# All four chunks' keys turned through VectorE and scratch memory, and two more gate pairs ahead of the projections, in a hybrid decoder layer

## The chip, the cores and the metric

One NeuronCore of a Trainium2 chip runs the whole program. The metric is the device time of one execution in microseconds (us). The profiled execution has a span (first to last recorded event) and, around it, a little time that is counted but not in the span.

## The reference

One decoder layer with model width 1024 is computed for a prompt of 2048 tokens and for 8 decode rows (one token each, with cached keys, values and state). Cut to what matters:

```
h    = rms_norm(x) * (1 + scale) + shift
proj = h @ w_in -> qa, ka, va, za, qb, fb, ib, zb
ya   = window_attention(rope(norm(qa)), rope(norm(ka)), va) * silu(za)      8 heads of 64, window 128
f    = lb + (1 - lb) * sigmoid(fb);  k = (1 - lb) * sigmoid(-fb)            4 heads of 128
per chunk:  o = (q * decay) @ S + A @ v;   S = decay_end * S + (k * decay_to_end)^T @ v
yb   = rms_norm(o) * silu(zb)
y    = sigmoid(h @ w_merge_a) * (ya @ w_proj_a) + sigmoid(h @ w_merge_b) * (yb @ w_proj_b)
out  = x + gate * (y @ w_out)
```

The outputs are the rows of both batches, the last 128 keys and values and the state S of each.

## The kernel before

**Passes, units, halves.** The prompt is done in four passes (`it` 0 to 3) of 512 tokens, each four chunks of 128. A pass is a list of 68 units (`UNITS`, line 36): products that fill one of two PSUM banks D0 and D1 in turn. Units 0 to 7 give q, k and v by token, then come four each of `za`, `f`, `qb`, `ib` and `zb` (8 to 27), then the list of `_merges()` (28 to 59), and eight units of the output projection (60 to 67). `ga j` and `gb j` are the gate units of output block j, `pa j` and `pb j` the projections of ya and yb. Each product is three matmuls (high by high, low by high, high by low part, lines 787 to 793), so a unit has 24 of them, a `pa` or `pb` unit 12. TensorE does a unit in two halves; half n stands for unit n // 2, half n % 2. Between halves it does the small tasks that a hand-written table puts there (`put`, `at_half`, lines 142 to 155), in four further PSUM banks XA to XD. Every engine walks the same table in the same order (line 998 on TensorE), does its own part of each task, and waits by semaphores.

**The recurrence's tasks.** After `level` 6 (unit 27) the decayed keys lie in `kk` with the key dimension on the partitions. `st` needs them the other way round. Two ways are in the kernel:

- Chunks 0 and 1: the task `KT` (line 971) turns a chunk with four TensorE transposes in units 28 and 29; ScalarE copies it to `kst` (line 1175).
- Chunks 2 and 3 (half 1, `KEYS_TURNED`): the task `kD` (line 1606) turns `kk` in place in blocks of 32 x 32 on VectorE. SyncE stores that half to the scratch memory `zk` (event `ks`, line 578) and reads it back with the blocks in exchanged places into `k_turned` (event `kl`, line 582, four loads).

Then for each chunk `o` (line 975, output) and `st` (line 986, state update) run on TensorE in banks XB and XA; VectorE adds to the state (line 1603), ScalarE copies `o` to `kk` and sums its squares (line 1180). `onorm` (line 1609) normalizes two chunks and turns them in blocks; SyncE takes them through scratch memory too (events `os`, `ol`). `yD` (line 1619) gates them, `yT` splits them in a high part (ScalarE, line 1222) and a low part (POOL, line 1782), which `pb 0` waits for (line 769). In pass 0 and 1 the constants O_AT, ON_AT, YD_AT, YT_AT give halves, KS_AT to OL_AT give unit numbers, equal in every pass.

**Weights.** A 512 KB block per unit is loaded by SyncE into one of three raw buffers (`weights`, line 535), split into a high part by ScalarE (line 1015) and a low part by POOL (line 1766). The unit at whose second half a block is split is planned (`SPOT`, line 114). SyncE issues block n once block n-3 has its low part and, where block n-3 takes part in a burst, once that burst is done. SyncE's queue is in order: its other transfers are events with a unit number as key, and an event is issued just before the block n with key <= max(SPOT[n-3], BURST_AT[n-3]) (line 688). An event that waits holds up all weight blocks behind it.

**Decode rows.** Their products use the raw blocks in bursts on TensorE in bank XD (task `bu`, lines 832 to 855; groups of four blocks, two blocks per burst, at BURST_AT). A burst waits for the landing of its blocks. One burst is that of ga1 and gb1, in the middle of unit 29 of pass 0. Sums follow one unit later (`sx`, VectorE and ScalarE). In pass 0 the cached keys and values of the decode rows are loaded (event `ckv`, line 636) into a buffer that ga1 and gb1's tanh used before, so it waits until VectorE has left pb1:

```
s.full(0, "PV", 3)
s.wait_ge("s_rows", 1)
s.unit_left(0, "pb", 1)
```

The keys are then turned by TensorE (`sT`, line 871) and used (`sS` to `sO`).

Of the kernel before, what the change touches and what calls it, by code (L numbers as in the profile page):

```python
# [16 lines left out]
P, KT, NT = 128, D // 128, TB // 128  # L17
HB = 4
# [8 lines left out]

def _merges():

    out = [(c, j) for j in range(5) for c in ("ga", "gb")]  # L30
    for j in range(8):
        out += [("pa", j), ("pb", j)] + [(c, {2: 5, 3: 6, 5: 7}[j]) for c in ("ga", "gb") if j in (2, 3, 5)]
    return out


# [94 lines left out]
        assert kind in ("q", "k", "v", "out") or _prev < _it * NU + FIRST_UNIT[_b] + (1 if _n in EARLY else 0), (_n, _prev)  # L130


KEYS_TURNED = (1,)
O_AT, ON_AT, YD_AT, YT_AT = (57, 59, 61, 63), (60, 64), (65, 66, 69, 70), (66, 67, 70, 71)
KS_AT, KL_AT, OS_AT, OL_AT = (28, 28), (28, 28), (30, 32), (31, 32)

AHEAD = {0: (), 1: (5, 7), 2: (1, 3, 5, 7), 3: (1, 3, 5, 7)}
AHEAD_AT = {1: 18, 3: 24, 5: 29, 7: 34}
# [22 lines left out]
for it in range(NIT):  # L161
    if it == 0:
        put(0, 3, 0, "gm", 0, "XA")
        put(0, 4, 1, "late", 0)
        put(0, 8, 0, "gb", 0, "XB")
        put(0, 8, 1, "gS", 0, "XC")
        put(0, 30, 0, "srow", 0)
    if it < 2:
        for _n, _g in enumerate(GROUPS[it]):
            for _b in _g:  # L170
                _s = BURST_AT[it * NB + _b] - it * NU
                if it * NB + _b in PAIR.values():
                    continue
                put(it, int(_s), int(2 * _s) % 2, "bu", _b, "XD", (it, "sg", _n))
            SAMPLE_SLOT[(it, _n)] = _s
    put(it, 2 if it else 20, 0, "at0", 0)
    for _t in range(NT):
        put(it, 2 + _t, 0, "qtB", _t, "XB" if _t % 2 else "XA")
        put(it, 6 + _t, 0, "qtA", _t, "XB" if _t % 2 else "XA")
    put(it, 3, 1, "rsk", 0)  # L180
    put(it, 5, 1, "kt", 0, "XA")
    put(it, 7, 1, "rsq", 0)
    for _n in range(8):
        at_half(it, S_AT[_n], "S", _n, None if _n in AHEAD[it] else "XA")
        at_half(it, S_AT[_n] + 1, "norm", _n)
    for _t in range(NT):
        at_half(it, PV_AT[_t], "PVa", _t, "XA")
        at_half(it, PV_AT[_t], "PV", _t, "XB")
        if _t < 3:
            at_half(it, PV_AT[_t], "turn", 2 * _t + 2)  # L190
    for _n in AHEAD[it]:
        at_half(it, AHEAD_AT[_n], "scores", _n, "XC", (it, "S", _n))
    if it == 0:
        put(0, 20, 0, "dg", 3, "XA", (0, "dg", 0))
    else:
        for _h in range(HB):
            at_half(it, (38, 38, 38, 40)[_h], "dg", _h, "XC", (it, "dg", 0))
    for _l in range(7):
        at_half(it, 42 + 2 * _l, "level", _l, "XA" if _l % 2 else "XB")
    for _t in range(NT):  # L200
        if _t // 2 not in KEYS_TURNED:
            put(it, 28 + _t, 0, "KT", _t, "XC")
        at_half(it, O_AT[_t], "o", _t, "XB")
        at_half(it, O_AT[_t], "st", _t, "XA")
    for _r in KEYS_TURNED:
        at_half(it, 56, "kD", _r)
    for _r in range(2):
        at_half(it, ON_AT[_r], "onorm", _r)
    for _t in range(NT):
        at_half(it, YD_AT[_t], "yD", _t)  # L210
        at_half(it, YT_AT[_t], "yT", _t)
    if it < NIT - 1:
        for _n, _t in enumerate((2, 3, 0, 1)):
            put(it, (41, 42, 45, 46)[_n], 1, "xst", _t)
        put(it, 48, 1, "rstd", 0)
        put(it, 52, 1, "bc", 0, "XA")
        for _n in range(4):
            put(it, (54, 56, 59, 60)[_n], 1, "xm", _n)
            put(it, (57, 58, 61, 62)[_n], 1, "hh", _n)
    if it == 0:  # L220
        for _n in range(11):
            _s = SAMPLE_SLOT[(0, _n)] + 1
            put(0, int(_s), int(2 * _s) % 2, "sy" if _n in (0, 1, 5) else "sx", _n, "XC")
        put(0, 33, 0, "sQ", 0, "XC")
        for _r in range(2):
            _u = (44, 52)[_r]
            put(0, _u, 0, "sT", _r, "XC"), put(0, _u + 1, 1, "sS", _r, "XC"), put(0, _u + 3, 0, "snorm", _r)
            put(0, _u + 4, 1, "sP", _r, "XC"), put(0, _u + 6, 0, "sO", _r, "XC")
    if it == 1:
        for _b in range(NS):  # L230
            put(1, _b + 1, 0, "vB", _b, "XD")
            put(1, _b + 2, 0, "so", _b, "XC", (1, "so", 0))
        put(1, 10, 1, "srms", 0)
        put(1, 13, 0, "soss", 0, "XC")
        for _n in range(6):
            _s = SAMPLE_SLOT[(1, _n)] + 1
            put(1, int(_s), int(2 * _s) % 2, "sx", _n, "XC")
            if _n >= 4:
                _s += 1 + (_n == 4)
                put(1, int(_s), int(2 * _s) % 2, "sOT", _n - 4, "XC")  # L240
# [13 lines left out]
SUMMED = {a: n + 1 for n, a in enumerate((2, 3, 6, 7, 8, 9, 10))}  # L254

TH = {(c, j): j for c in ("za", "f", "zb") for j in range(4)}
TH.update({(c, j): (4, 6, 0, 2, 8, 0, 2, 0)[j] + (c == "gb") for j in range(8) for c in ("ga", "gb")})
TH_PREV, _last = {}, {}
for _it in range(NIT):
    for _u in UNITS:  # L260
# [71 lines left out]
def build(nc, A, O):  # L332

    ctx = ExitStack()
    with ctx:
# [136 lines left out]
        pb = {}  # L472
# [47 lines left out]
        def _(sp):  # L520
# [26 lines left out]
            for it in range(NIT):  # L547
                b0 = it * NU
                if it < NIT - 1:
                    later.setdefault(b0 + 33, []).append(("xst", it, 0))  # L550
                    later.setdefault(b0 + 43, []).append(("x01", it, 0))
                    later.setdefault(b0 + 48, []).append(("xh", it, 0))
                    later.setdefault(b0 + (50 if it else 59), []).append(("xh", it, 1))
                later.setdefault(b0 + 5, []).append(("vr", it, 0))
# [9 lines left out]
                        later.setdefault(b0 + 60 + t, []).append(("out1", it, t))  # L564
                    later.setdefault(b0 + 64 + t, []).append(("out", it, t))
            later.setdefault(3, []).append(("win", 0, 0))
            later.setdefault(41, []).append(("ckv", 0, 0))
            later.setdefault(50, []).append(("ckv", 0, 1))
            later.setdefault(NU - 1, []).append(("sst", 0, 0))
            for b in range(NS):  # L570
                later.setdefault(NU + b + 2, []).append(("sso", 1, b))
# [134 lines left out]
        def _(pe):  # L706
# [90 lines left out]
            def side(it, task, a, key):  # L797
# [160 lines left out]
                elif task == "PV":  # L958
                    s.wait_ge("p_norm", 8 * it + 2 * a + 2)
                    s.wait_ge("vr", 96 * (it + 1))  # L960
                    for j in range(5):
                        for i in range(4):
# [5 lines left out]
                                         start=j == 0, stop=j == 4)  # L968
                            if (i, j) == (1, 4):
                                s.done(ins, "XA_full")  # L970
                elif task == "KT":
                    s.wait_ge("lvl", 8 * it + 8)
                    for h in range(HB):
                        ins = tr(bank[:, P * h:P * h + P], kk[:, h, P * a:P * a + P], ident[:, :])
                elif task == "o":
                    s.freed(it, "level", 6)
                    s.unit_left(it, "ib", a)
# [6 lines left out]
                        ins = mm(bank[:, P * h:P * h + P], AT[:, h, P * a:P * a + P], ibtok[:, a, P * h:P * h + P],  # L984
                                 start=not more, stop=True)
                elif task == "st":
                    if a < 2:
                        s.freed(it, "KT", a)
                    else:
                        s.wait_ge("kt_in1", 64 * (it + 1))  # L990
                    for h in range(HB):
                        left = kst[:, h, :] if a < 2 else k_turned[:, 1, h, a % 2, :]
                        ins = mm(bank[:, P * h:P * h + P], left, ibtok[:, a, P * h:P * h + P],  # L993
                                 start=True, stop=True)
                if PARTS[key][-1] == (task, a):
                    s.done(ins, f"{b}_full")
# [10 lines left out]
        def _(act):  # L1007
# [114 lines left out]
            def side(it, task, a, key):  # L1122
# [47 lines left out]
                elif task == "S":  # L1170
# [1 line left out]
                        s.wait_ge("smax", 2 * (8 * it + a) + m // 2 + 1)  # L1172
                        fn(p_t[:, m, :], p_t[:, m, :], ACT.Exp, bias=negm[:, m:m + 1], accum_out=rsum[:, m:m + 1])  # L1173
                    s.done(fn(esk, esk, ACT.Exp), "p_exp")
                elif task == "KT":
                    s.full(*key)
                    if a:
                        s.full(it, "st", a - 1)
                    s.free(fn(kst, bank[:, :].rearrange("p (h n) -> p h n", h=HB), ACT.Copy), *key)
                elif task == "o":  # L1180
                    s.full(*key)
                    if it or a:
# [731 lines left out]
```

## Time and profile before

| | |
|---|---|
| median of 3 runs | 1548.65 us (1546.63 to 1549.49) |
| the profiled execution | 1547.77 us |
| its span | 1545.6 us |
| TensorE (PE) busy | 1514.8 us, 98% |
| VectorE (DVE) busy | 824.8 us, 53% |
| ScalarE (ACT) busy | 535.9 us, 35% |
| POOL busy | 828.8 us, 54% |

In the rows PE is the matmul side of TensorE and SPq the queue of SyncE. Times are in us from the start of the span where a row begins with one, `x` is a count, and what follows the last bar or stands in brackets is idle time of that engine just before, with what ended it. L983 is line 983 of the kernel. A matmul's duration overlaps the next one's start, so what one costs is read from start to start.

### The profile page before, as it was taken

How to read it: one execution, taken by the hardware profiler on the slowest of the kernel's cores; microseconds unless marked ns; L12 is line 12 of the kernel's file. 1: busy time of each engine (PE TensorE's matmuls, PEld its weight loads, DVE VectorE, ACT ScalarE, POOL GpSimd, SP SyncE). 2: the span in 40 equal slices, each digit the busy share in tenths (PEclk: the TensorE clock that was granted, in tenths of full speed). 3: DMA queues.
4: the chain of work that ended last, by engine and by line, in shares of the span. 5: the costliest groups of instructions: out<-in, count | busy, mean ns of one | idle time of the engine just before them, and what ended most of it. 6: DMA issues, size and time to landing. Idle time of an engine off the chain costs nothing.

```text
span 1545.6 us, 31555 instructions
## 1 busy us (share of the span) xinstructions
PE 1514.8 (98%) x12936; PEld 1232.8 (80%) x12936; DVE 824.8 (53%) x1971; ACT 535.9 (35%) x1112; POOL 828.8 (54%) x1074
## 2 busy tenths in 40 slices
PE   6999999999999999999999999999999999999998
PEld 3777788777887777887779878888888977788886
DVE  5766465236578856434444774642453775642123
ACT  4334323443313432334231452243432352243330
POOL 1525433658854633366683482447795372437671
PEclk9999999999999999999999999999999999999999
DMA  9612213534463311443343331345543231244351
GB/s 365 234 42 85 82 57 94 166 127 160 163 208 113 108 59 59 133 138 136 122 166 124 101 113 42 95 119 171 176 165 136 77 110 56 71 125 124 106 170 58
DMA packets 119047, 191.52 MB, mean 124 GB/s; under 512 B 57198, under 2 KB 74951, under 8 KB 118120
## 3 DMA queue, kind: packets, MB, share of 16 engines
q1 hardware_dynamic: 118480, 189.34, 37.3%
q8 instruction: 102, 1.67, 0.4%
q14 instruction: 41, 0.34, 0.1%
q10 hardware_dynamic: 424, 0.17, 0.0%
HBM read 169.13 MB, written 18.25 MB: 121 GB/s over the span
## 4 chain that ended last, share of the span: by engine, by line
PE 93%; DVE 3%; SPq 1%; issue 1%; DMA 1%; ACT 1%; DVEq 0%
PE ps_D L793 55%; PE ps_D L790 25%; PE ps_XCD L855 1%; PE ps_XB L931 1%; SPq L524 1%; PE ps_XA L956 1%; PE ps_XA L967 1%; PE ps_XA L993 1%; PE ps_XB L984 1%; PE ps_XB L983 1%; PE ps_XA L931 1%; DMA th_t<-in_w_ada 1%; PE ps_XB L967 1%; PE ps_XCD L956 0%; PE ps_XCD L866 0%
## 5 line engine op out<-in xcount | busy, mean ns | idle before, releaser
L1766 POOL TENSOR_TENSOR w_lo_t<-w_raw,w_hi_t 128x256 fp32r<-128x256 f32 x920 | 685.2, 778 | 588.3 <-ACT w_hi_t L1015 588.0
L793 PE MATMUL ps_D<-h_hi_t,w_hi_t 128*128 128x512 f32 x1024 | 409.1, 399 | 0.0
L793 PE MATMUL ps_D<-h_lo_t,w_hi_t 128*128 128x512 f32 x1024 | 399.4, 390 | 0.0
L793 PE MATMUL ps_D<-h_hi_t,w_lo_t 128*128 128x512 f32 x1024 | 399.3, 390 | 0.0
L1015 ACT ACTIVATE w_hi_t<-w_raw 128x1024 fp32r<-128x1024 f32 x232 | 240.0, 1051 | 116.1 <-PE ps_D L790 62.0
L793 PEld LDWEIGHTS ps_D<-h_hi_t,w_hi_t 128*128 128x128 f32 x1024 | 192.2, 188 | 48.0 <-issue 10.0
L793 PEld LDWEIGHTS ps_D<-h_hi_t,w_lo_t 128*128 128x128 f32 x1024 | 192.2, 188 | 41.3
L793 PEld LDWEIGHTS ps_D<-h_lo_t,w_hi_t 128*128 128x128 f32 x1024 | 192.5, 188 | 36.9
L790 PE MATMUL ps_D<-w_hi_t,h_hi_t 128*128 128x384 f32 (+1 forms) x384 | 141.4, 368 | 1.4 <-DVE yf_t L1400 1.0
L790 PE MATMUL ps_D<-w_hi_t,h_lo_t 128*128 128x384 f32 (+1 forms) x384 | 136.5, 355 | 0.0
L790 PE MATMUL ps_D<-w_lo_t,h_hi_t 128*128 128x384 f32 (+1 forms) x384 | 136.3, 355 | 0.0
L790 PE MATMUL ps_D<-w_hi_t,y_hi_t 128*128 128x512 f32 x256 | 100.2, 391 | 2.2 <-issue 2.2
L790 PE MATMUL ps_D<-w_hi_t,y_lo_t 128*128 128x512 f32 x256 | 99.6, 389 | 0.0
L790 PE MATMUL ps_D<-w_lo_t,y_hi_t 128*128 128x512 f32 x256 | 99.6, 389 | 0.0
L790 PEld LDWEIGHTS ps_D<-w_hi_t,h_hi_t 128*128 128x128 f32 x384 | 72.6, 189 | 12.0 <-issue 4.9
L1514 DVE TENSOR_TENSOR qq<-qq,ff 128x1024 f32<-128x1024 f32 x28 | 40.8, 1458 | 70.5 <-PE ps_XB L931 47.1
L1173 ACT ACTIVATE p_or_hf<-p_or_hf,sm 128x160 f32<-128x160 f32 x128 | 53.3, 418 | 68.8 <-DVE sm L1561 67.4
L790 PEld LDWEIGHTS ps_D<-w_hi_t,h_lo_t 128*128 128x128 f32 x384 | 72.6, 189 | 5.1 <-issue 0.5
L790 PEld LDWEIGHTS ps_D<-w_lo_t,h_hi_t 128*128 128x128 f32 x384 | 72.5, 189 | 5.3
L1452 DVE TENSOR_TENSOR acc_or_kst<-ps_D,gate_bc 128x512 f32<-128x512 f32 x32 | 22.1, 692 | 99.6 <-PE ps_D L790 99.6
L1097 ACT ACTIVATE th_t<-ps_D,bm_half 128x512 f32<-128x512 f32 x40 | 27.6, 690 | 132.5 <-PE ps_D L793 132.5
L1603 DVE SCALAR_TENSOR_TENSOR state<-state,ff,ps_XA 128x128 f32<-128x128 f32 x64 | 17.9, 342 | 79.2 <-PE ps_XA L993 79.2
(390 smaller groups left out, 2338.5 us busy)
## 6 DMA issues: line engine op xcount, KB each, us to landing
w_raw<-in_w_blocks SPq DMA_DIRECT2D x232, 512.0 KB, 3.4
xr<-in_x_prompt SPq DMA_DIRECT2D x16, 512.0 KB, 5.1
x_or_AT<-in_x_prompt SPq DMA_DIRECT2D x14, 512.0 KB, 5.0
out_dram<-xr SPq DMA_DIRECT2D x12, 512.0 KB, 2.9
z_o<-kk SPq DMA_DIRECT2D x8, 512.0 KB, 3.1
x_or_AT<-in_x_turned SPq DMA_DIRECT2D x3, 1024.0 KB, 5.7
p_or_hf<-in_x_turned SPq DMA_DIRECT2D x3, 1024.0 KB, 5.7
z_k<-kk SPq DMA_DIRECT2D x4, 512.0 KB, 4.7
```

The source lines that it names most:

```text
L524: s.done(sp.dma_start(dst, src, **kw), name, by=16)
L790: ins = mm(bank[:, 0:P * nb].rearrange("p (n c) -> p n c", c=P), a[:, k, P * j:P * j + P], w[:, s0:s0 + nb, k, :], start=go, stop=end)
L793: ins = mm(bank[:, :], w[:, s0, k0 + k, :], a[:, k, :], start=go, stop=end)
L931: ins = mm(bank[row:row + left, m * col:m * col + m], kk[:, h, c + 32 * g:c + 32 * g + left], right, start=True, stop=True)
L967: ins = mm(dst[DH * g:DH * g + DH], val[:, DH * g:DH * g + DH], PT[r, g, :, 32 * j:32 * j + 32], start=j == 0, stop=j == 4)
L1015: s.done(fn(w_hi[:, SLOT[n % NB]], w_raw[:, n % NRAW], ACT.Copy), "w_hi")
L1097: s.leave(fn(dst, bank[:, :], ACT.Tanh, scale=0.5, bias=bm_half[:, c:c + 1]), it, u)
L1173: fn(p_t[:, m, :], p_t[:, m, :], ACT.Exp, bias=negm[:, m:m + 1], accum_out=rsum[:, m:m + 1])
L1452: leave(tt(acc[:, 0:w], bank[:, 0:w], gate_bc[:, c0:c0 + w], ALU.mult), it, u)
L1514: s.done(tt(qr, qr, fl[:, :, :, 0:1].broadcast_to(shape), ALU.mult))
L1603: ins = stt(state[:, h, :], state[:, h, :], ff[:, h, P * a:P * a + 1], bank[:, P * h:P * h + P], ALU.mult, ALU.add)
L1766: ins = g_.tensor_tensor(w_lo[:, c, k:k + 2], w_raw[:, n % NRAW, k:k + 2], f32(w_hi[:, c, k:k + 2]), ALU.subtract)
```

## The change

It does four things. The merge list puts ga5 and gb5 behind gb4, so the projections begin two units later (pa0 is unit 40 instead of 38, pb0 41, pa1 42, pb1 43, pa2 44), and ga6, gb6 stay units 48 and 49, ga7, gb7 become 52 and 53. The keys of both halves go through `kD`, `ks` and `kl`; `KT` is gone on TensorE and ScalarE, and `st` waits for the landing of its half's loads. The tasks `o` to `yT` move some halves later, the key stores get the key 27 instead of 28 and the key loads 27.1, the output stores and loads 32 and 34. Tasks of the next pass's x tiles and of the decode rows move by one or two units, and the tanh of ga5, gb5 gets the buffers 10 and 11.

```diff
-    out = [(c, j) for j in range(5) for c in ("ga", "gb")]
+    out = [(c, j) for j in range(6) for c in ("ga", "gb")]
     for j in range(8):
-        out += [("pa", j), ("pb", j)] + [(c, {2: 5, 3: 6, 5: 7}[j]) for c in ("ga", "gb") if j in (2, 3, 5)]
+        out += [("pa", j), ("pb", j)] + [(c, {3: 6, 4: 7}[j]) for c in ("ga", "gb") if j in (3, 4)]
...
-KEYS_TURNED = (1,)
-O_AT, ON_AT, YD_AT, YT_AT = (57, 59, 61, 63), (60, 64), (65, 66, 69, 70), (66, 67, 70, 71)
-KS_AT, KL_AT, OS_AT, OL_AT = (28, 28), (28, 28), (30, 32), (31, 32)
+KEYS_TURNED = (0, 1)
+O_AT, ON_AT, YD_AT, YT_AT = (61, 63, 65, 67), (64, 68), (72, 73, 76, 77), (73, 74, 77, 78)
+KS_AT, KL_AT, OS_AT, OL_AT = (27, 27), (27.1, 27.1), (32, 34), (32.1, 34.1)
...
-            put(it, (41, 42, 45, 46)[_n], 1, "xst", _t)
-        put(it, 48, 1, "rstd", 0)
+            put(it, (43, 44, 46, 47)[_n], 1, "xst", _t)
+        put(it, 49, 0, "rstd", 0)
...
-            _u = (44, 52)[_r]
+            _u = (45, 53)[_r]
...
-TH.update({(c, j): (4, 6, 0, 2, 8, 0, 2, 0)[j] + (c == "gb") for j in range(8) for c in ("ga", "gb")})
+TH.update({(c, j): (4, 6, 0, 2, 8, 10, 0, 2)[j] + (c == "gb") for j in range(8) for c in ("ga", "gb")})
...
-                    later.setdefault(b0 + 43, []).append(("x01", it, 0))
+                    later.setdefault(b0 + 44, []).append(("x01", it, 0))
...
-            later.setdefault(41, []).append(("ckv", 0, 0))
-            later.setdefault(50, []).append(("ckv", 0, 1))
+            later.setdefault(42, []).append(("ckv", 0, 0))
+            later.setdefault(51, []).append(("ckv", 0, 1))
...
-                elif task == "KT":
-                    s.wait_ge("lvl", 8 * it + 8)
-                    for h in range(HB):
-                        ins = tr(bank[:, P * h:P * h + P], kk[:, h, P * a:P * a + P], ident[:, :])
...
-                    if a < 2:
-                        s.freed(it, "KT", a)
-                    else:
-                        s.wait_ge("kt_in1", 64 * (it + 1))
+                    s.wait_ge(f"kt_in{a // 2}", 64 * (it + 1))
                     for h in range(HB):
-                        left = kst[:, h, :] if a < 2 else k_turned[:, 1, h, a % 2, :]
-                        ins = mm(bank[:, P * h:P * h + P], left, ibtok[:, a, P * h:P * h + P],
+                        ins = mm(bank[:, P * h:P * h + P], k_turned[:, a // 2, h, a % 2, :], ibtok[:, a, P * h:P * h + P],
                                  start=True, stop=True)
...
-                elif task == "KT":
-                    s.full(*key)
-                    if a:
-                        s.full(it, "st", a - 1)
-                    s.free(fn(kst, bank[:, :].rearrange("p (h n) -> p h n", h=HB), ACT.Copy), *key)
```

## Rows read from the trace of the kernel before

**Rows 1.** The page, part 1: busy us (share) and instructions of each engine.

```profile
PE 1514.8 (98%) x12936; PEld 1232.8 (80%) x12936; DVE 824.8 (53%) x1971; ACT 535.9 (35%) x1112; POOL 828.8 (54%) x1074
```

**Rows 2.** Waits of PE: who waited for whom, us in total, times, longest.

```profile
PE ps_D L790 <- issue: 2.6, 2, 2.2
...
PE ps_XB L983 <- ACT yf_t L1189: 1.3, 1, 1.3
```

**Rows 3.** Timeline of ACT, pass 2, units 34 and 35: start, us, what.

```profile
1045.96 0.69 ACT L1097 ACTIVATE th_t<-ps_D,bm_half 128x512 f32<-128x512 f32 x1 [3.29 <-PE ps_D L793]
...
1051.40 0.69 ACT L1097 ACTIVATE th_t<-ps_D,bm_half 128x512 f32<-128x512 f32 x1 [3.29 <-PE ps_D L793]
```

**Rows 4.** Groups of PE instructions: busy us, mean ns, idle before.

```profile
L974 PE MATMUL ps_XCD<-ident,kk 128*128 128x128 f32 x32 | 4.8, 273 | 0.0
```

**Rows 5.** Timeline of PE, pass 2, around the task KT 0.

```profile
998.64 0.60 PE L974 MATMUL ps_XCD<-ident,kk 128*128 128x128 f32 x4
...
999.31 0.40 PE L793 MATMUL ps_D<-h_lo_t,w_hi_t 128*128 128x512 f32 x1
```

**Rows 6.** Timeline of DVE, pass 0, the task kD.

```profile
241.62 1.25 DVE L1608 STREAM_TRANSPOSE kk<-kk 128x1024 f32<-128x1024 f32 x1
```

**Rows 7.** Timeline of PE, pass 0: KT 0 in unit 28, burst in unit 29.

```profile
240.78 0.38 PE L974 MATMUL ps_XCD<-ident,kk 128*128 128x128 f32 x2
...
248.60 1.07 PE L855 MATMUL ps_XCD<-w_raw,hS_or_yS 128*32 128x256 f32 x16
```

**Rows 8.** SPq issues with median landing (windows 234:236, 239:240, page part 6); timelines of SPq and ACT.

```profile
w_raw<-in_w_blocks SPq DMA_DIRECT2D x1, 512.0 KB, 3.2
...
239.39 0.33 SPq L524 DMA_DIRECT2D w_raw<-in_w_blocks  x1
...
w_raw<-in_w_blocks SPq DMA_DIRECT2D x1, 512.0 KB, 4.8
...
z_k<-kk SPq DMA_DIRECT2D x4, 512.0 KB, 4.7
...
289.52 0.86 SPq L524 DMA_DIRECT2D w_raw<-in_w_blocks  x2
...
295.71 1.06 ACT L1015 ACTIVATE w_hi_t<-w_raw 128x1024 fp32r<-128x1024 f32 x1 [1.33 <-DMA w_raw<-in_w_blocks]
```

**Rows 9.** Timeline of SPq, pass 0, key loads; landing of all loads of k_turned.

```profile
246.05 2.84 SPq L524 DMA_DIRECT2D k_turned<-z_k  x4
...
DMA to landing us min/median/max: 2.7/3.0/4.0
```

**Rows 10.** Timelines of PE and SPq, pass 0: the cached keys, both rounds.

```profile
321.96 0.39 PE L793 MATMUL ps_D<-w_hi_t 128*128 128x512 f32 x1
...
327.34 1.38 SPq L524 DMA_DIRECT2D p_or_hf<-out_dram  x2
...
331.88 0.60 PE L874 MATMUL ps_XCD<-ident,p_or_hf 128*128 128x128 f32 x4
...
366.50 1.23 SPq L524 DMA_DIRECT2D p_or_hf<-out_dram  x2
...
369.02 0.63 PE L874 MATMUL ps_XCD<-ident,p_or_hf 128*128 128x128 f32 x4
```

**Rows 11.** Timeline of POOL, pass 2, unit 35: split and low part.

```profile
1053.12 2.82 POOL L1766 TENSOR_TENSOR w_lo_t<-w_raw,w_hi_t 128x256 fp32r<-128x256 f32 x4 [1.38 <-ACT w_hi_t L1015]
1055.90 1.28 POOL L1782 TENSOR_TENSOR yb_lo_t<-yf_t,yb_hi_t 128x512 fp32r<-128x512 f32 x1
```

**Rows 12.** Windows of PE: us, busy (count), granted clock, DMA share, GB/s.

```profile
34.00:36.00 2.00, 0.17 (x2) 0.60 0.53 183
...
41.00:44.00 3.00, 3.00 (x21) 0.96 1.03 420
...
1541.00:1543.00 2.00, 0.00 (x0) 1.00 0.31 120
...
775.00:785.00 10.00, 7.76 (x48) 1.00 0.83 311
```

## The prediction, made before the changed kernel was run

> **What bounds the kernel now.** I read the page's busy line first: TensorE is busy 1514.8 of 1545.6 us, 98% [rows 1]. No other engine comes near, so a change moves the time only by taking work off TensorE or by opening or closing a gap in it. Then TensorE's own waits [rows 2]: past the opening there are few, and two matter here, a gap of 1.3 us in front of line 983 (products `o` of chunk 3, first pass) and one of 2.2 us in pass 1 ahead of unit 60, which nothing in this change touches. So this is a sum of TensorE time removed and of new TensorE waits. DMA landings, VectorE and ScalarE count only where TensorE reaches something before it is there; for that I walked the order of each queue before and after.
>
> One unit of 24 matmuls takes 5.44 us: ScalarE's evacuations of two neighbouring units start at 1045.96 and 1051.40 [rows 3]. A half is 2.72 us, a matmul 0.227 us; `pa` and `pb` units have 12 matmuls, 2.72 us.
>
> **Part 1, what goes.** Eight `KT` tasks (chunks 0 and 1 in four passes), four TensorE transposes each: 32 instructions, 4.8 us busy in the group [rows 4]. But busy counts a pipelined tail. One task starts at 998.64 and the second dense matmul behind it starts at 999.31 [rows 5]; without the task it would start 0.227 us after 998.64, at 998.87. So a task costs 0.44 us, eight cost 3.5 us, and I take that; 4.8 us is the upper bound. ScalarE's eight copies out of the bank go too, off the path, and so do `st`'s waits for them. `o` and `st` cost the same at their new places.
>
> **Part 2, the wait that goes.** The 1.3 us of [rows 2] came from ScalarE being late: it stood behind the decode rows' sums (`sx` 7), which VectorE did only after the long `srow` and `onorm` 0, all in unit 30. Now `onorm` 0 is in unit 32, and `srow` starts on an idle VectorE right after the key transposes. I book -1.3 us; nothing would be the other bound.
>
> **Part 3, what comes to VectorE.** One more `kD` per pass, 1.25 us [rows 6]. VectorE has nothing else until `st` 0, which moves from half 57 to 61. Cost nothing; without that cover it would be 5.0 us.
>
> **Part 4, the key stores now stand ahead of a weight block.** This is the first new wait. SyncE's queue is in order. The stores had key 28 and stood behind the loads of gb1 and ga2 in pass 0; with key 27 both stand in front of them, because the burst of gb0 is at unit 27. In pass 0 the decode rows use raw weights too: the burst of the pair ga1, gb1 (line 855) stands on TensorE in the middle of unit 29 and waits for gb1's raw block to land. Before, it was out ahead of the block issued at 239.39 [rows 8], and TensorE reached the burst at 248.60 [rows 7]. Now: `kD` 0 from 241.62 to 242.87, `kD` 1 until about 244.15, the second store issued to about 244.8, then gb1 at 244.8. Landing takes 3.2 us (a lone block), 4.8 us (the block at 239.39), or 6.2 us where two tiles of 512 KB stood ahead (issued 289.52, ScalarE got it at 295.71); the scattered stores themselves take 4.7 us at the median [rows 8]. I take 4.8, so 249.6. TensorE is there earlier than before, without `KT`, `o` and `st`: the half-unit that followed `KT` 0 can start at 240.78 [rows 7], plus two halves, 246.2. The wait is 3.4 us; bounds 1.8 and 4.8. ScalarE's split of gb1 waits as well (queued behind it: the evacuation of unit 29, which comes later anyway); POOL then finishes the low part at about 254, and unit 31 needs it at about 259. In passes 1 to 3 there is no burst in these units; the block held back there (gb2) has its split at unit 30 and costs nothing.
>
> **Part 5, the loads back.** `st` 0 now waits for k_turned half 0. The store issued behind `kD` 0 at 242.9 lands 4.7 us later [rows 8]; four loads are issued over 2.84 us and land at most 4.0 us after issue [rows 9]. So 242.9 + 4.7 + 2.8 + 4.0 is 254.4. In a pass without bursts TensorE reaches `st` 0 five halves and one `o` (about 1.8 us) after 240.78, at 256.2. It costs nothing, with 2 us to spare; the eight loads hold SyncE some 3 us more, and the next block (gb2 or ga3) is due units later. The loads read runs of 128 B, and the landing of each at a median of 3.0 us is no longer than a weight block's [rows 8, 9]. The Trainium skill ("DMA: Bandwidth & Descriptors", Specifications) says that runs under 512 B do not reach line rate; by that the loads could take twice as long and `st` 0 would wait 2 or 3 us a pass, and the trace disagrees, since half of these very loads are already in it.
>
> **Part 6, the cache rows of the decode batch.** This is the second new wait, in pass 0 alone. The load of the cached keys (`ckv` 0) waits until VectorE has left pb1, since it overwrites ga1 and gb1's tanh. Putting ga5 and gb5 ahead moves pb1 from unit 41 to 43, but the TensorE transposes that read the keys (`sT` 0) move only from unit 44 to 45. Before, the unit behind pb1 begins at 321.96, VectorE empties pb1's bank, SyncE starts the loads, and the last two are issued from 327.34 to 328.72, and `sT` runs at 331.88, 9.9 us after 321.96 and without a wait [rows 10]. In the second round the last two are issued from 366.50 to 367.73 and `sT` 1 runs at 369.02 unhindered [rows 10], so a landing takes at most 1.3 us more: ready at 330.0, 8.0 us after the unit behind pb1 begins. Now between the two lie pa2 (2.72) and half of pb2 (1.36), 4.1 us. The wait is 4.0 us; bounds 2.7 (landed with the issue) and 5.8 (landed just before 331.88). The second round gets more room, a whole ga7 unit.
>
> **Part 7, the tail of yb.** pb0 in unit 41 waits for POOL's low part of chunk 3, now at unit 39 instead of 35. By the pattern of [rows 3, 11], counted from the end of unit 38: split on POOL from +1.7 to +4.5, then two low parts of 1.28 us, +7.1; TensorE reaches pb0 at +8.2. Nothing, with 1 us to spare; if POOL were 2 us late in each pass it would be 4 us. `onorm` 1 to `yD` 2 grows from 5 to 8 halves, which ends VectorE's waits for the outputs' round trip; they were off the path. SyncE's tile and weight loads behind the moved output stores (`os`, `ol` 0 and 1, `x01`) keep at least 2 us before each reader.
>
> **The sum:** -3.5 - 1.3 + 3.4 + 4.0 = +2.6 us. The profiled execution took 1547.77 us, so 1550.4; the median of the runs is 0.9 higher, which gives **1551.3 us** against 1548.65. With all bounds one way it is -1.6, the other way +6.9.
>
> **Rivals.** *The clock falls (slower, 1554.3).* Place: the two new waits of 3 to 4 us in pass 0. In the opening the granted clock fell in the stretch 34 to 36, where TensorE was busy 0.17 of 2 us (a mean of 0.60 puts 1.6 us of it at the lower level, 1.2 GHz), and 41 to 44 has a mean of 0.96, so it was back at 2.4 GHz by 41.2 [rows 12]: 6.8 us at half clock. Price: with at least 1.8 us of these idle, 2.5 us were lost, and 3.4 had work filled them; I take 3.0. The point where it decides: a gap of 2.2 us in pass 1 [rows 2] lies in the window 775 to 785, which is at full clock, and so is 1541 to 1543, with no matmul [rows 12]. Waits of 3.4 and 4.0 us are longer than either, and no row shows on which side they fall. The Trainium skill ("TensorE: Matmul & The Clock Gate", Why this matters for your kernels) advises against idle gaps of a few microseconds between bursts of matmuls for this reason, and the trace agrees with its direction.
>
> *One of the two waits is hidden (no change, 1547.3 to 1547.9).* For the first: DMA engines are under half busy there, the block may land 3.2 us after issue and leave 1.8. For the second nothing but a misread order speaks.
>
> *Both are hidden (faster, 1543.8).* Then only -4.8 is left. It needs both orders to be misread; the low TensorE share of waits today speaks for a program whose covers are wide, the counted halves against it.
>
> **Chances:** my sum 0.36, the clock 0.28, one wait 0.20, none 0.14, something else 0.02. A measurement here can tell about 0.2%, 3.1 us, from no change. My sum sits at +2.6, and four tenths of it lies beyond +3.1 (0.15); with nearly all of the clock case and the rest that is slower 0.43. Both hidden, and a little of one hidden, is faster 0.15; same 0.42. The range takes in both hidden at 1543.8 and the clock case with a long wait: 1543.5 to 1556. The range of my sum alone is 1547.0 to 1555.6.
>
> **What would show it.** TensorE's list of waits gains one on the burst of line 855 near 246 us, released by a weight DMA, and one on line 874 near 330 us, released by the cache loads; the one of line 983 is gone; 32 transposes of line 974 are gone. Without the two waits my sum is wrong and the time falls by 4 to 5 us. A window right behind either wait with a granted clock near 0.5 is the clock rival. A wait of line 993 on k_turned, or of a `pb` unit on yb_lo, in several passes would be a cost that I set to nothing.

## The result, and the profile after

| | time, us | runs |
|---|---|---|
| before | 1548.48 median (1546.63 to 1549.49) | 4 |
| after | 1557.71 median (1555.97 to 1558.76) | 4 |

The ratio is 1.006, with a 95% interval of 1.0044 to 1.0076: slower by 9.2 us. The forecast was 1551.3, in a range that ended at 1556. The profiled execution of the changed kernel took 1558.76 us (span 1556.6).

TensorE is still what the kernel hangs on; part 1 of the page has 32 instructions fewer on it, as meant [rows 1]:

```profile
PE 1518.9 (98%) x12904; PEld 1234.1 (79%) x12904; DVE 826.1 (53%) x1975; ACT 531.0 (34%) x1104; POOL 831.5 (53%) x1074
```

Busy TensorE grew by 4.1 us although 32 transposes went, so something ran slower. The waits of PE (us in total, times, longest), against [rows 2]:

```profile
PE ps_XCD L874 <- DMA p_or_hf<-out_dram: 3.9, 1, 3.9
PE ps_XCD L913 <- issue: 3.4, 2, 1.7
PE ps_XCD L855 <- DMA w_raw<-in_w_blocks: 3.3, 1, 3.3
...
PE ps_D L793 <- DVE yf_t L1434: 1.3, 1, 1.3
...
PE ps_D L790 <- issue: 0.7, 1, 0.7
```

Both new waits of the prediction are there, at 3.3 and 3.9 us against 3.4 and 4.0. The 1.3 us of line 983 is gone, and the gap of 2.2 us ahead of line 790 is down to 0.7. One wait was not foreseen: 1.3 us in front of pb7 of pass 0 (line 793, on VectorE).

The first wait on the timelines of SPq and PE, which answer to [rows 7, 8, 9] (start, us, what). The stores are issued first, gb1 and ga2 behind them from 245.26. The last dense matmul ahead of the burst starts at 246.44, and the burst goes 4.9 us after the issue of its block:

```profile
243.34 1.82 SPq L524 DMA_DIRECT2D z_k<-kk  x2
245.26 1.30 SPq L524 DMA_DIRECT2D w_raw<-in_w_blocks  x2
246.61 8.97 SPq L524 DMA_DIRECT2D k_turned<-z_k  x8
```

```profile
246.44 0.39 PE L793 MATMUL ps_D<-h_hi_t,w_lo_t 128*128 128x512 f32 x1
250.12 1.93 PE L855 MATMUL ps_XCD<-w_raw,hS_or_yS 128*32 128x256 f32 x16 [3.29 <-DMA w_raw<-in_w_blocks]
...
252.58 0.63 PE L793 MATMUL ps_D<-h_lo_t,w_hi_t 128*128 128x512 f32 x1
253.01 0.63 PE L793 MATMUL ps_D<-h_hi_t,w_lo_t 128*128 128x512 f32 x1
```

The 16 matmuls of the burst took 1.93 us where they took 1.07 before [rows 7], and the dense matmuls behind it start 0.43 us apart (252.58, 253.01) in place of 0.227. The same behind the second wait, which answers to [rows 10]:

```profile
344.35 1.37 SPq L524 DMA_DIRECT2D p_or_hf<-out_dram  x2
```

```profile
347.02 1.08 PE L874 MATMUL ps_XCD<-ident,p_or_hf 128*128 128x128 f32 x4 [3.86 <-DMA p_or_hf<-out_dram]
```

The windows of PE (us, busy with its count, granted clock, DMA share, GB/s), against [rows 12]:

```profile
249.60:252.00 2.40, 1.88 (x17) 0.50 1.03 255
252.00:256.00 4.00, 4.00 (x14) 0.50 0.89 140
256.00:260.00 4.00, 4.00 (x21) 0.95 1.01 297
...
346.00:350.00 4.00, 2.98 (x9) 0.50 0.79 252
350.00:356.00 6.00, 6.00 (x37) 0.84 0.22 65
...
580.00:584.00 4.00, 4.00 (x13) 0.58 0.02 4
```

A granted clock of 0.50 is 1.2 GHz. It fell behind both waits, for 6.8 us each time (249.6 to 256.4 and about 345.2 to 352.0), and a third time for 3.4 us near 580 in pass 1, behind a gap of 1.7 us that nothing released. In the kernel before, no window between 42 and 1543 us lies under 1.00.

**The account.** From 40 to 1490 us, TensorE stood idle for 1450 less its busy time, in the kernel before and in the changed one:

```profile
40.00:1490.00 1450.00, 1438.86 (x12577) 1.00 0.37 118
```

```profile
40.00:1490.00 1450.00, 1432.10 (x12496) 0.99 0.38 120
```

That is 11.1 and 17.9 us: +6.8. Half clock over 17.0 us of the trace costs at most half of it, 8.5. The transposes give 3.5 back. Sum +11.8 at most, or +10.6 without the 2.4 us of half clock that passed while TensorE still stood; the spans differ by 11.0 (the medians by 9.2: the other three executions of the changed kernel had mean clocks of 0.993 to 0.995, the profiled one 0.991).

The medians can be compared too. Each execution has its mean granted clock on record, to 0.001. One less that clock, times the span, is the most that half clock can have cost. This "clock loss" is 10.5 us on average in the changed kernel's four executions, and 4.6 us in 92 executions of the kernel before. So 6.8 of idle time, 5.9 of clock loss and -3.5 of transposes give +9.2 at most and +8.0 without the same 1.2 us, where 9.2 was measured.

The 6.8 are the two waits (7.2) and pb7's (1.3), less line 983's (1.3); the small gaps in pass 1 and behind it cancel within 0.4.

### The profile page after: what moved, and what is told of

Its sections match the earlier page's. It is cut to its first block, busy times and chain, and to the rows that moved or that the text cites. A ratio compares the mean times of both kernels' runs of the same rounds, so it can differ in the third digit from the quotient of the medians.

```text
span 1556.6 us, 31505 instructions
## 1 busy us (share of the span) xinstructions
PE 1518.9 (98%) x12904; PEld 1234.1 (79%) x12904; DVE 826.1 (53%) x1975; ACT 531.0 (34%) x1104; POOL 831.5 (53%) x1074
## 3 DMA queue, kind: packets, MB, share of 16 engines
q8 instruction: 102, 1.67, 0.5%
## 4 chain that ended last, share of the span: by engine, by line
PE 92%; DVE 4%; DMA 1%; SPq 1%; issue 1%; ACT 0%; DVEq 0%
PE ps_D L793 54%; PE ps_D L790 25%; PE ps_XCD L855 2%; SPq L524 1%; PE ps_XB L931 1%; PE ps_XB L980 1%; PE ps_XA L985 1%; PE ps_XA L956 1%; PE ps_XA L967 1%; PE ps_XB L979 1%; PE ps_XA L931 1%; DMA th_t<-in_w_ada 1%; PE ps_XB L967 0%; PE ps_XCD L956 0%; PE ps_XCD L866 0%
## 5 line engine op out<-in xcount | busy, mean ns | idle before, releaser
L793 PEld LDWEIGHTS ps_D<-h_hi_t,w_hi_t 128*128 128x128 f32 x1024 | 193.0, 188 | 50.1 <-issue 11.8
L1089 ACT ACTIVATE th_t<-ps_D,bm_half 128x512 f32<-128x512 f32 x32 | 22.0, 689 | 116.5 <-PE ps_D L793 116.5
```

What stands on the lines that cost most here:

```text
L793: ins = mm(bank[:, :], w[:, s0, k0 + k, :], a[:, k, :], start=go, stop=end)
L1089: s.leave(fn(dst, bank[:, :], ACT.Tanh, scale=0.5, bias=bm_half[:, c:c + 1]), it, u)
```

## The experiments

Twelve kernels ran, in four groups, each beside its own executions of the kernel before (1547.68, 1547.96, 1548.77 and 1547.89 us). "Cover" is the TensorE work that lies between a transfer's start and its reader, and hides it. Where an edit adds lines, the line numbers behind it are that many higher. "Idle" below is worked out as above, from each profiled execution's busy time from 40 to 1490 us; "clock loss" is the average over all executions of a kernel, as above, and good to some 0.5 us.

**1. Take the two waits away one at a time, then both.** The first edit puts gb1's load ahead of the key stores in pass 0, the second moves the transposes of the cached keys in the first round from half 90 to half 92:

```diff
-                        later.setdefault(b0 + KS_AT[r], []).append(("ks", it, r))
+                        later.setdefault(b0 + KS_AT[r] + (0 if it else 0.05), []).append(("ks", it, r))
```

```diff
-            put(0, _u, 0, "sT", _r, "XC"), put(0, _u + 1, 1, "sS", _r, "XC"), put(0, _u + 3, 0, "snorm", _r)
+            at_half(0, (92, 2 * _u)[_r], "sT", _r, "XC"), put(0, _u + 1, 1, "sS", _r, "XC"), put(0, _u + 3, 0, "snorm", _r)
```

*The first edit alone:*

> The changed kernel, but in pass 0 the key stores stand behind the loads of gb1 and ga2 again. Theory (each of the two new waits costs its own length and then 6.8 us at half clock): the burst's wait of 3.3 us near 246 is gone and so is the half clock behind it, 6.7 us less than the changed kernel's 1557.7, about 1551; the wait of 3.9 us on the cached keys and 6.8 us of half clock behind it stay. Rival A (the clock falls for another reason): only 3.3 us less, 1554.4, and two stretches of half clock stay. Rival B (the time is lost in the longer way of the keys or in the later yb): no more than 3 us less, and waits of st on k_turned or of pb on yb_lo in the list.

*The second alone:*

> The changed kernel, but the transposes of the first four cached keys stand in unit 46, behind the burst, not in unit 45. Theory: cover grows from 4.1 to 7.9 us, so the wait of 3.9 us shrinks to under 0.3 and the half clock behind it goes: 7.3 us less than 1557.7, about 1550.4. Rival A (clock falls for another reason): 3.9 less, 1553.8. Rival B: no more than 3 us less.

*Both:*

> Both edits together. Theory: 14 us less than 1557.7, about 1543.7, faster than the kernel before by 0.3%; the granted clock is at half level only in the opening and after the end, as before. Rival A: 7.2 us less, 1550.5, half-clock stretches stay. Rival B (the moves themselves cost): it stays above the kernel before's 1548.5.

| kernel | wait left | median, us | ratio to before (95%) |
|---|---|---|---|
| gb1 ahead of the stores | L874, 3.9 | 1550.25 | 1.0016 (1.0006 to 1.0026) |
| cached keys read later | L855, 3.3 | 1549.67 | 1.0023 (1.0013 to 1.0033) |
| both | none | 1543.82 | 0.9979 (0.9970 to 0.9987) |

Each edit took away its wait and nothing else of size. Against the last kernel a wait of 3.9 us costs 6.4 us, one of 3.3 us costs 5.9, and both together 13.9 (1557.71 less 1543.82, from two groups): each wait costs itself and about 3 us more. So the changed kernel with its covers is 4 us faster than the kernel before, and the two lost covers turn that into a loss. How much of the 4 us is the change itself stays open, since experiment 6 moves as much by position alone.

The times are as expected, the stretches of half clock not quite. With gb1 ahead of the stores, 6.8 us of half clock were expected behind the wait of 3.9 us, and the profiled execution has 3.4 (the changed kernel has 6.8 behind the same wait). The profiled executions of the other two have another stretch of 3.4 us in pass 1, although with both covers half clock was expected in the opening and at the end only. Clock loss is 6.8, 7.7 and 4.1 us in the three kernels. It differs between executions of one kernel: with gb1 ahead, the fastest (1548.11) has a mean clock of 0.998 and the slowest (1552.53) 0.994. So the 3 us over a wait are an average.

**2. Double and shrink one wait.** Three kernels with both covers, except that the cached keys' transposes are at half 91, 89 or 87 (the first of the two numbers in the second edit).

> The kernel with both covers restored, with the cached keys' transposes one half earlier (half 91; the changed kernel has them at 90, where the wait on the cache loads was 3.9 us and the time 6.4 us over the kernel with both covers, 1543.8). The wait should be 3.9 less one half of a pb unit, 1.36: about 2.6 us. Theory (a wait costs itself, and the stretch behind it is at half clock for up to 6.8 us, so up to 3.4 us more, once the wait is about 3 us or longer; a wait of 2.2 us left the clock alone in the kernel before): 1546.4 if the clock stays, 1549.8 if it falls, and I expect it to stay. Rival (the wait alone costs, and the rest of the 6.4 us was something else): 1546.4 in either case, with no stretch at half clock near it.

> The same with the cached keys' transposes at half 89, one half earlier than in the changed kernel. The wait should be 3.9 + 1.36 = 5.3 us. Theory (wait, and one stretch of half clock worth up to 3.4 us, however long the wait): 1543.8 + 5.3 + up to 3.4 = 1549.1 to 1552.5, a window of about 0.5 granted clock behind the wait, and the point value 1552. Rival A (the wait alone): 1549.1 with no such window. Rival B (the clock's price grows with the wait, 2.5 us at a wait of 3.9): 1543.8 + 5.3 x 1.64 = 1552.5.

> The same with the cached keys' transposes at half 87, right behind pb1. The wait should be 3.9 + 3 x 1.36 = 8.0 us. Theory (wait, and a stretch of half clock worth up to 3.4 us, however long the wait; where half clock is granted while TensorE still waits it costs nothing): 1551.8 to 1555.2. Rival A (the wait alone): 1551.8 with no window near 0.5 over busy matmuls. Rival B (the clock's price grows in proportion to the wait): 1543.8 + 8.0 x 1.64 = 1556.9.

| wait of L874 | median, us | over 1543.82 | less the wait |
|---|---|---|---|
| 2.56 (half 91) | 1548.88 | 5.1 | 2.5 |
| 3.89 (half 90, from above) | 1550.25 | 6.4 | 2.5 |
| 5.25 (half 89) | 1552.26 | 8.4 | 3.2 |
| 7.94 (half 87) | 1555.14 | 11.3 | 3.4 |

The ratios to before are 1.0004 (0.9994 to 1.0015), 1.0027 (1.0017 to 1.0037) and 1.0046 (1.0029 to 1.0062). The waits came to within 0.1 us of what was expected. I expected the clock to stay in the shortest (1546.4), and it fell there too, the miss of this series: windows of PE with half 91,

```profile
338.00:342.00 4.00, 1.64 (x8) 1.00 0.23 69
342.00:346.00 4.00, 3.80 (x22) 0.67 0.72 261
346.00:350.00 4.00, 4.00 (x25) 0.90 0.57 196
```

and with half 87:

```profile
334.00:338.00 4.00, 0.00 (x0) 1.00 0.45 133
338.00:342.00 4.00, 1.09 (x5) 0.50 0.30 98
342.00:346.00 4.00, 4.00 (x13) 0.65 0.44 169
```

With 7.94 us of wait (333.0 to 340.9) half clock was granted from 338.0 to 344.8, and 2.9 us of it cost nothing, since TensorE was still waiting. With 2.56 us it came only 1.2 us after the matmuls had begun again, at 343.4. So in the medians the price over a wait does not grow in proportion: 2.5 to 3.4 us while the wait triples. Clock loss over that of the kernel with both covers agrees: 1.8, 2.7, 4.0 and 4.7 us in the four rows, of which 1.3 and 1.5 us in the last two rows (by the profiled executions) fell on a TensorE that was still waiting. That the wait alone costs would give ratios of 0.9990, 1.0000, 1.0007 and 1.0025 in the four rows, each below its interval, at half 91 and 87 by little. For the proportional price the intervals are too wide (1556.9 is inside at half 87), and only the windows and the clock loss speak against it: 3.4 us of matmuls at half clock at half 91, 3.9 at half 87.

**3. Fill the waits.** If it is TensorE's standing still that costs the extra, work that computes nothing, put into the wait, must take the extra away although the wait stays. In front of the wait on the cache loads:

```diff
                 elif task == "sT":
+                    if a == 0:
+                        for n in range(15):
+                            mm(bank[:, 0:512], h_hi[:, 0, 0:P], h_hi[:, n % KT, :], start=True, stop=True)
                     s.wait_ge("ckv", 64 * (a + 1))
```

and in the changed kernel also in front of the wait on gb1:

```diff
+                    if it == 0 and BLOCKS[a] == ("gb", 1):
+                        cf = GROUPS[it][key[2]].index(a) - 1
+                        for m in range(26):
+                            mm(bank[:, P * cf:P * cf + 256], h_hi[:, 0, 0:P], h_hi[:, m % KT, 0:256], start=True, stop=True)
                     s.wait_ge(f"w_in{n % NRAW}", came[n])
```

*Into the kernel of the first experiment's first line, where only L874 waits:*

> The kernel in which only the wait on the cache loads is left (gb1 ahead of the stores; 1550.25, with a wait of 3.9 us), with 15 matmuls of 128x512 that compute nothing in front of that wait, into the bank that the transposes then overwrite: 15 x 0.227 = 3.4 us of the 3.9 are filled, the rest stays idle. The transposes start when they did. Theory (2.5 us of the 6.4 over the kernel with both covers, 1543.8, are the clock, which falls because TensorE stands still): no window near 0.5 behind line 874, a wait of about 0.5 us, and 1543.8 + 3.9 = 1547.7. Rival (the clock has no part, the 2.5 us come of the later transposes or of something else): 1550.2, as without the filling.

*Into the changed kernel, both:*

> The changed kernel (1557.7) with both of its new waits filled in the same way: 26 matmuls of 128x256, about 2.9 us, in front of the wait of line 855 on gb1's raw block (3.3 us), and 15 of 128x512, 3.4 us, in front of the wait of line 874 on the cache loads (3.9 us). Theory: no stretch at half clock behind either; what is left over the kernel with both covers is 3.3 + 3.9 = 7.2 us, so 1551.0, and 6.7 us of the changed kernel's time were the clock's. Rival (waits alone are the cost, and the rest of the 13.9 us between the two kernels lies elsewhere): 1557.7, unchanged by the filling.

The changed kernel with both waits filled took **1546.51 us** (ratio 0.9982, 0.9973 to 0.9990), 11.2 us less than without the 41 useless matmuls. No half clock is left behind either wait; its timeline and windows of PE:

```profile
248.55 3.27 PE L838 MATMUL ps_XCD<-h_hi_t 128*128 128x256 f32 x26
252.37 1.07 PE L859 MATMUL ps_XCD<-w_raw,hS_or_yS 128*32 128x256 f32 x16 [0.54 <-DMA w_raw<-in_w_blocks]
```

```profile
252.00:260.00 8.00, 7.63 (x47) 1.00 0.93 165
...
346.00:354.00 8.00, 7.47 (x48) 1.00 0.62 211
```

The burst again takes 1.07 us. But 1546.5 is 4.5 us under what I expected, and the other kernel, 1549.88 (1.0008, 0.9999 to 1.0017), is 2.2 over: its wait was filled and the clock stayed at 1.00 there, yet its time is hardly under the 1550.25 without the filling. By the time alone the rival (1550.2) would stand. The idle time tells why it does not. Without the waits themselves, idle TensorE is 9.1 us in the kernel with gb1 ahead of the stores (13.0 less 3.9), 11.1 in the same one filled (11.8 less 0.7), 10.7 in the changed kernel, and 5.8 in it filled (7.0 less 1.2). The gaps that changed are those with no releaser: 3.4 us of line 913 in the changed kernel, none when filled; 0.8 us ahead of line 790 with gb1 ahead, 2.1 when filled, and there the clock fell afterwards. Timeline and windows of PE there:

```profile
783.09 0.56 PE L790 MATMUL ps_D<-w_hi_t,y_hi_t 128*128 128x512 f32 x1 [2.14 <-issue]
```

```profile
782.00:786.00 4.00, 2.91 (x7) 0.67 0.98 390
```

Clock loss, over all executions, shows the filling at work in both: 6.8 us before and 3.9 after it with gb1 ahead, 10.5 and 4.2 in the changed kernel; the kernel with both covers has 4.1. With it both times come out, closer even than the 0.5 us that these figures are good to. Gb1 ahead: -2.9 of clock, -1.2 of idle time, and 15 matmuls at 0.227 us, +3.4, make -0.7, and -0.4 was measured. Both waits: -6.3, -10.9 and about +6.3 for the two fillings make some -11, and -11.2 was measured. And of the eleven executions with one wait filled, the three with a mean clock of 0.999 took 1548.15 to 1548.82 us, near the expected 1547.7, and the four with 0.996 took 1550.96 to 1551.92. So the clock's part is shown, and a second effect of up to 5 us, which had nothing to do with the waits, lay over it.

**4. The crowd on VectorE.** The kernel with both covers, with xm 0 one unit earlier:

```diff
-                put(it, (54, 56, 59, 60)[_n], 1, "xm", _n)
+                put(it, (53, 56, 59, 60)[_n], 1, "xm", _n)
```

> The kernel with both covers restored, and VectorE's first scaling of the next pass's rows (xm 0) in unit 53 instead of 54, in every pass. Theory: the wait of 1.3 us of line 793 on VectorE's yf_t (pb7 of pass 0) comes of VectorE being crowded in units 54 to 59, now six short units in a row; with one task earlier it goes, and the time is 1543.8 - 1.3 = 1542.5. Rival: what makes VectorE late there is the decode rows' snorm 1 alone, and the wait stays at 1.3: 1543.8. A third way: xm 0 in front of the bc bank's reader delays TensorE elsewhere and the time rises.

1543.54 us (ratio 0.9970, 0.9958 to 0.9982). PE's wait of 1.3 us on yf_t ahead of pb7 is gone from its list, and idle is 8.0 us against 9.6. The rival (snorm 1 alone) is out. The time itself is 1.0 over what was expected and is not told apart from 1543.82, which is of another group.

**5. The keys back on TensorE.** With both covers restored, `KT` of chunks 0 and 1 returns, with its reader and ScalarE's copy as before the change, in units 30 and 31, and then with KT 0 in unit 28:

```diff
-KEYS_TURNED = (0, 1)
+KEYS_TURNED = (1,)
...
+            put(it, 30 + _t, 0, "KT", _t, "XC")
```

```diff
-            put(it, 30 + _t, 0, "KT", _t, "XC")
+            put(it, (28, 31)[_t], 0, "KT", _t, "XC")
```

> As the one before it, but the keys of chunks 0 and 1 are turned by TensorE again (in units 30 and 31), so the reordering of the gates alone is left of the change. Theory: eight tasks at 0.44 us, 3.5 us more than e3, about 1547.2, 1.3 under the kernel before for the wait of line 983 that went. If the busy time were the price it is 4.8 more, 1548.5. Rival (the way through scratch memory costs what it saves): no difference to e3.

> The kernel with both covers and the keys of chunks 0 and 1 back on TensorE, as in the fourth run, with the two KT tasks in units 28 and 31 in place of 30 and 31, so that KT 0 no longer shares the bank and the half of the decode rows' sx 7. In the fourth run (1551.05) the keys cost 7.2 us where 3.5 was priced: 0.9 a pass in passes 2 and 3, but 2.0 and 2.6 in passes 0 and 1, with a wait of 0.7 us of line 866 and a gap of 2.3 us ahead of unit 60. Theory: the 0.7 us goes and 1550.3 is left, since the gap ahead of unit 60 of pass 1 stays. Rival (that gap goes with the instructions' places, as it did between the earlier kernels): a gap of 0.7 instead of 2.3, no half clock behind it, and 1547.3 to 1548.7.

1551.05 us (1.0024, 1.0014 to 1.0034), then 1549.5 (1.0007, 0.9999 to 1.0016): 7.2 and 5.7 us over 1543.82, where 3.5 was priced. Part of the first is the place I gave KT 0: it shared bank and half with the decode rows' sums, and line 866 waited 0.7 us for ScalarE; in unit 28 that wait is gone. In passes 2 and 3 the stretch from the first zb unit (24) to the output projection (unit 60) is 1.0 and 0.6 us longer with the keys on TensorE (170.11 and 169.21 us against 169.12 and 168.59), where two tasks of 0.44 make 0.9. The rest is in gaps without a releaser (idle 11.2 and 10.7 against 9.6), the one ahead of line 790 in pass 1 above all, and in the clock (loss 5.4 and 4.9 against 4.1): 3.5 + 1.6 + 1.3 is 6.4 of the 7.2, and 3.5 + 1.1 + 0.8 is 5.4 of the 5.7. With the keys in 28 and 31 the gap ahead of line 790 stayed, as expected, but the clock did not fall behind it, which was not. Timeline of PE with the keys in 30 and 31, and its windows:

```profile
781.70 0.47 PE L790 MATMUL ps_D<-w_hi_t,y_hi_t 128*128 128x512 f32 x1 [2.28 <-issue]
```

```profile
782.00:786.00 4.00, 4.00 (x12) 0.60 1.02 417
```

Here a gap of 2.3 us was followed by a fall of the clock; with the keys in 28 and 31 one of 2.14 us was not,

```profile
780.99 0.47 PE L790 MATMUL ps_D<-w_hi_t,y_hi_t 128*128 128x512 f32 x1 [2.14 <-issue]
```

```profile
782.00:786.00 4.00, 4.00 (x19) 1.00 1.02 414
```

nor was one of 2.2 us in the kernel before [rows 2, 12]. But the gap of experiment 3 at the same place, also 2.14 us, was.

**6. Move the instructions and nothing else.** What fills and keys have in common is that they shift every later instruction of TensorE. So the kernel of experiment 4 got 41 tiny transposes in the opening, where TensorE waits anyway:

```diff
             s.done(ins, "p_T")
+            for k in range(20):
+                tr(pb["XB"][:, 0:9], R2[0:9, 0:P], ident[0:9, 0:9])
             s.wait_ge("p_c", 1)
...
+                for k in range(21 if (it, t) == (-1, 2) else 0):
+                    tr(bank[:, 0:9], R2[0:9, 0:P], ident[0:9, 0:9])
                 s.wait_ge("xn", 4 * (it + 1) + t + 1)
```

> The kernel with both covers and xm 0 in unit 53 (1543.54; idle TensorE from 40 to 1500 us: 8.0), with 41 transposes of 9x9 that compute nothing in TensorE's own waits of the opening (20 behind the first group of line 711, 21 ahead of line 741's wait). They put every later instruction of TensorE 41 places further back, as the 41 filling matmuls did in the changed kernel with both waits filled, in which the gaps with no releaser ahead of lines 913 and 931 in pass 1 (3.0 and 1.2 us) were absent. Theory (those gaps hang on where an instruction lies in the program, and not on the data it waits for): they go here too, 2.5 to 4 us off, 1539.5 to 1541, if the opening hides the 41 (about 2.5 us in gaps of 0.9, 1.7 and 2.4 us). Rival (in that kernel they were hidden by something else, such as TensorE being late against the decode rows' work): the gaps stay and the time is 1543.5 to 1545.

**1539.76 us** (1538.73 to 1541.81; ratio 0.9948, 0.9935 to 0.9962): the fastest kernel of the study, 0.5% under the kernel before, and inside the 1539.5 to 1541 expected. Windows of PE over the gaps of pass 1 and over the whole, first without the 41,

```profile
560.00:570.00 10.00, 8.50 (x203) 1.00 0.16 56
...
590.00:600.00 10.00, 9.38 (x163) 1.00 0.17 56
```

```profile
40.00:1490.00 1450.00, 1442.00 (x12568) 1.00 0.37 121
```

then with them:

```profile
560.00:570.00 10.00, 9.94 (x209) 1.00 0.16 56
...
590.00:600.00 10.00, 10.00 (x290) 1.00 0.19 57
```

```profile
40.00:1490.00 1450.00, 1446.19 (x12594) 1.00 0.38 122
```

Idle fell from 8.0 to 3.8 us, by 4.2, and the median by 3.8. The gaps of lines 913 and 931 in passes 1 and 2 are gone, with the same work, data and waits around them. So it is shown that adding instructions far ahead of these gaps takes them away. That it is the instruction's place in the program that counts fits this kernel and the changed one with 41 matmuls added, but one number of added instructions was tried in the opening, and the mechanism is not shown. The page of the profile counts instruction DMAs of 1.67 MB in all these kernels, but I found no row that ties one of them to one gap.

## Why the prediction was wrong

**Part 1 (-3.5) and part 2 (-1.3) held.** Two `KT` tasks a pass were priced at 0.9 us, and the stretch from the first zb unit to unit 60 got 1.0 us shorter in the undisturbed passes (170.11 to 169.12 in pass 2, before and after, 169.21 to 168.26 in pass 3). Putting them back cost 5.7 to 7.2, of which the part over 3.5 is mostly idle time in other places and the clock (experiment 5). Line 983 waits no more.

**Parts 4 and 6 (3.4 and 4.0) held** in place, releaser and size, 3.3 and 3.9. The estimates that carried them were sound: gb1 was ready 4.9 us after its issue (4.8 was taken from the block at 239.39 [rows 8]), and the cached keys' transposes went 1.3 us behind the last issues (345.72 to 347.02), the 1.3 read off the second round [rows 10].

**Parts 3, 5 and 7 cost nothing**, as written: no wait of TensorE on VectorE's key transposes, on k_turned or on yb's low part is in the list. The loads of k_turned landed like this:

```profile
DMA to landing us min/median/max: 2.8/3.3/5.7
```

The median rose from 3.0 to 3.3 [rows 9] with twice as many, and `st` 0 did not wait in any pass. Part 5 weighed the rule of the Trainium skill's "DMA: Bandwidth & Descriptors" (Specifications) that runs under 512 B do not reach line rate, and took from it an estimate of 2 to 3 us of wait a pass. The trace has no such wait.

**The failed step is the clock.** The sum took it at nothing, with no row for that side, and it stood outside as a rival with 0.28, in one fall of 3.0 us. The text reasoned that waits of 3.4 and 4.0 us are longer than a gap of 2.2 that had left the clock alone, "and no row shows on which side they fall". It fell behind both, and in the profiled execution of every kernel with a wait on line 855 or 874 of 2.56 us or more (the changed kernel, and five of the experiments). The price over the wait was 2.5 to 3.4 us in the medians each time, so two falls were due, not one. Filling both waits took 6.3 us of clock loss away. With 2 x 3 added, the sum of +2.4 as the waits came out would have been 8.4, of 9.2 measured. The rival was right in mechanism and a factor of two short in count: nothing in the argument made the second wait's fall less likely than the first's. The upper bound of the sum was also added up wrong, without consequence: -3.5 + 4.8 + 5.8 is +7.1, not +6.9. "TensorE: Matmul & The Clock Gate" of the Trainium skill (Why this matters for your kernels) advises against idle gaps of a few microseconds between bursts, and experiments 2 and 3 agree.

**Missed: pb7's 1.3 us.** Six short units (pa5 to pb7) now stand in a row, and VectorE gets a bank to empty every 2.72 us there while it still has the decode rows' sums and the next pass's rows. Part 7 asked what VectorE waits for, not how much lies on it between 388 and 408 us. Experiment 4 takes the wait away.

**Not foreseen, and in no part: position.** Idle TensorE beside the waits on DMA discussed here came to anything from 3.8 to 11.2 us, mostly gaps without a releaser, and moved with the edits. Between the kernel before and the changed one it nearly cancels (9.8 us beside the wait of line 983, 9.4 beside the three new waits), so it doesn't explain this result, but it is most of the +2.2 and -4.5 us by which experiment 3 missed (+1.5 and -3.8 us, against the 9.6 us of the kernel with both covers).

**Still open:** why the clock fell behind gaps of 2.28 and 2.14 us and not behind another of 2.14 and one of 2.2; why the same wait of 3.9 us was followed by 3.4 us of half clock in one kernel and 6.8 in another; the third fall near 580 us, behind a gap of 1.7 us. Two more kernels (both covers; cached keys read later) have a fall at that place, behind 1.85 us, and the one with the keys at half 87 has one in pass 2 (near 948 us), behind 1.58 us, while the one with the keys at half 91 has a gap of 1.7 us and none.

## What to carry to other kernels

In this kernel, with TensorE 98% busy, each wait of 2.56 us or more cost itself and some 3 us behind it. So price such waits with a fall of the clock in the sum, one for each of two waits that lie 97 us apart. If a wait can't be moved away, matmuls that compute nothing in front of it can keep the clock up (they took 2.9 and 6.3 us of clock loss away here), but look at the whole time: with one wait filled the median fell by 0.4 us only. And before 3 us are credited to an edit, take the gaps without a releaser out of both traces: 41 small instructions added in an idle stretch of the opening were worth as much (3.8 us) as the changed kernel with its covers gains over the kernel before (3.9 us).

## What the runs showed of the hardware that I had not expected

The granted clock fell and rose apart from the wait's own ends: it went to half 1.2 us after work had begun again (wait of 2.56 us), or while TensorE still stood (3.29, 3.86, 5.25 and 7.94 us), and stayed there for 3.4 or 6.8 us. Two gaps of 2.14 us at the same place of two kernels went either way. And 41 tiny transposes in the opening, some 4.7 us of TensorE's own instructions, took 4.2 us of idle time out of the passes behind it, most of it in passes 1 and 2 (1543.54 to 1539.76 us).
